# Gate and output chunks of three mixers in the wide form: 512 + 256 columns and a sum on VectorE

## The chip, the cores and the metric

One core of a Trainium2 chip runs the kernel. The metric is the device time of one execution in microseconds; before the change it is 2266.87 us, the median of three runs (2266.55 to 2266.92).

## What is computed

Two blocks over a sequence of 256 tokens of 1024 features, in float32. The first has an even and an odd mixer, each followed by a SwiGLU; the second has two layers of SwiGLU, layer norm, hybrid mixer, layer norm, SwiGLU, layer norm. The change touches the gate of the odd mixer and the last product of the hybrid mixers:

```python
def odd_mixer(h, w_in, out_norm, w_out, pos):
    z = h @ w_in
    ...
    g = z[..., 2 * nq + nv:]
    o = rmsnorm(retention(q, k, v), out_norm)
    o = o.reshape(B, S, nv).astype(h.dtype) * jax.nn.silu(g)
    return o @ w_out

def hybrid_mixer(x, w_in, ...):
    ...
    merged = (gates[:, :, 0] * (o_a @ w_br_a) + gates[:, :, 1] * (o_b @ w_br_b)
              + gates[:, :, 2] * (o_c @ w_br_c))
    return merged @ w_out
```

## The kernel before

Activations lie feature-major: 128 features on the partitions, 256 tokens along the free axis, 8 such tiles for 1024 features. Weights stream through the core once, in chunks of 128 x 1024 values that one output tile of 128 features needs, in the order of the list `ORDER`. SyncE loads a chunk into one of six raw buffers. ScalarE rounds it to the high part `whi` (`upper`, L1239) and VectorE forms the low part `wlo` = raw - high (`lower`, L2001), each in one of five buffers; a buffer comes free when the chunk five before it has been multiplied. Activations have a high and a low part too, side by side in `m.xx` (the hybrid mixer's merged tensor in `m.mx`).

A product is high x high + low x high + high x low. TensorE has two forms for it.

- Narrow (`mm3`, L454, used by `gemm_fm`, L471): per k step three matmuls of 256 columns into the same 256 columns of a PSUM bank: high weights by high activations, low weights by high, high weights by low. Three weight loads. One operand of the reader then holds the whole result.
- Wide (`mm2`, L459, used by `gemm_wide`, L480): per k step one matmul of 512 columns (high weights by both parts of the activations, side by side) and one of 256 (low weights by the high part). Two weight loads. The result is the sum of the two halves of a bank, which the reader has to add: by a reduction on VectorE (`both`, L1997), or, where it is added to the residual x, by two instructions (`add_wide`, L2037) in place of one (`add_one`, L2047).

`gemm_first` (L487) interleaves several output tiles over k, so that a stage can start on the first tiles of its input. `take` (L445) makes TensorE wait for the last reader of a PSUM bank before it is written again.

Each engine has a program of its own, whose order is written out by hand; they meet at semaphores. Where a mixer has work beside its weight chunks, it is put into generators that are advanced by one step after each chunk (`Sides`, L151), on each engine for itself.

**The odd mixer.** Its gate has 16 chunks `ow_g`, TensorE loop at L900, into banks 0 to 3 in turn. For chunk i VectorE (L2761) lowers a weight chunk, waits for the product, multiplies it by the row of 1/rms (L2774) and advances its generators; ScalarE raises a weight chunk and applies SiLU (L1680). Beside this run the four retention heads: head 0 begins at i = 0, head 1 at i = 7, head 2 at i = 14, head 3 in the output product. For a head, TensorE forms the scores at its first step and the outputs two steps later, for which it needs VectorE's product with the decay (L2732, L2733), and the sum of squares two steps after that, for which it needs VectorE's sum of ScalarE's squares (L1656, L1659, L2739, L2742). Later VectorE forms the reciprocal (L2757), the scaled outputs (L2749), their product with the gate (L2753) and their low part (L2022). The output product `ow_out` follows with `gemm_acc` (L525): its first chunk writes banks 0 to 3, two tiles to a bank, and takes each bank as it comes to it, after the last reader of gate chunks 12 to 15.

**The hybrid mixer.** In its last stage TensorE multiplies the eight chunks `mw_o`: tiles 0 to 2 interleaved by `gemm_first`, tiles 3 to 7 one by one (L1203). VectorE adds each tile to x (`norm_tile` with `add_one`, L3124) and prepares the layer norm in the same loop (L2124): after tile 2 it lowers three weight chunks, subtracts an estimate of the mean from all eight tiles (L2150, L2153) and forms the low parts of the raw input of the next stage (L2193); for tiles 3 to 7 it adds, lowers a weight chunk and forms a low part; after tile 7 it forms seven partial sums (L2180) and seven partial sums of squares (L2188) and one more low part. ScalarE squares the tiles and forms their high parts. TensorE goes on to the feed-forward stage on the raw input (`gemm_raw`, L578), whose k steps wait for those low parts, and after two tiles it forms the mean (`layer_norm`, L569), for which it waits for the last partial sum.

Of the kernel before, what the change touches and what calls it, by code (L numbers as in the profile page):

```python
# [433 lines left out]
def tensor_program(e, m):  # L434
# [10 lines left out]
    def take(b, *readers):  # L445
        for sig, *key in free[b]:
            w.wait_ge(s[sig], *key)
        free[b] = list(readers)
        return ps[b]
# [9 lines left out]
    def mm2(b, wh, wl, a, start):  # L459

        mm(b[:, :], wh, a.rearrange("p a b -> p (a b)"), start=start, stop=False)
        return mm(b[:, 0:256], wl, a[:, 0, :], start=False, stop=True)
# [8 lines left out]
    def gemm_fm(name, i, out, ah, al, st=None):  # L471
        wh, wl = weights(name, i)
        for k in range(8):
            if st is not None:
                w.wait_ge(s["xlo"], st, k)
            c = k * 128
            t = mm3(out, wh[:, c:c + 128], wl[:, c:c + 128], ah[:, k, :], al[:, k, :], k == 0, k == 7)
        t.then_inc(s["gemm"].h, s["gemm"].up(name, i))

    def gemm_wide(name, i, b):  # L480
        wh, wl = weights(name, i)
        for k in range(8):
            c = k * 128
            t = mm2(b, wh[:, c:c + 128], wl[:, c:c + 128], m.xx[:, k], k == 0)
        t.then_inc(s["gemm"].h, s["gemm"].up(name, i))

    def gemm_first(st, specs, wide=False, a=m.xx, last=None):  # L487

        wv = []
        for k in range(8):  # L490
            if k == 6 and last:
                last()
            w.wait_ge(s["xlo"], st, k)
            for n, (name, i, out) in enumerate(specs):
                if k == 0:
                    wv.append(weights(name, i))
                wh, wl = wv[n]
                c = k * 128
                if wide:
                    t = mm2(out, wh[:, c:c + 128], wl[:, c:c + 128], a[:, k], k == 0)  # L500
                else:
                    t = mm3(out, wh[:, c:c + 128], wl[:, c:c + 128], a[:, k, 0, :], a[:, k, 1, :], k == 0, k == 7)
                if k == 7:
                    t.then_inc(s["gemm"].h, s["gemm"].up(name, i))
# [356 lines left out]
    def odd():  # L861
        for cg in range(4):
            bq = [take(2 * (cg % 2) + tt, ("ract", "v", cg, tt)) for tt in range(2)]
            gemm_tm("ow_v", cg * 4, bq, xh, xl, 8, 2, 512, st="o")
            if cg == 0:
                rms_stats("o", RT=True)
        for i in range(8):
            for c in (2 * i, 2 * i + 1):
                gemm_wide("ow_qk", c, take(4 + c % 4, ("rdve", "qk0", c)))
        hb = [h1, h2]  # L870

        def head(h):
            w.wait_ge(s["rdve"], "qk", 2 * h + 1)
            b = take(5, ("rdve", "A", h))
            for d in range(2):
                mm(b[:, 0:256], m.okF[:, 2 * h + d, 0:128], m.oqF[:, 2 * h + d, :], start=d == 0, stop=d == 1)
            for d in range(2):
                t = mm(b[:, 256:384], m.okF[:, 2 * h + d, 128:256], m.oqF[:, 2 * h + d, 128:256], start=d == 0, stop=d == 1)
            t.then_inc(s["rps"].h, s["rps"].up("A", h))
            yield  # L880
            yield
            w.wait_ge(s["rdve"], "A", h)
            w.wait_ge(s["ract"], "v", 3, 1)
            for pr in range(2):
                b = take(6 + pr, ("ract", "o", h, pr))
                for q in range(2):
                    ec = h * 512 + (pr * 2 + q) * 128
                    ob = b[:, q * 256:q * 256 + 256]
                    mm(ob, m.ovT[:, 0, ec:ec + 128], m.oAT[:, h % 2, 0:256], start=q == 0, stop=False)
                    t = mm(ob[:, 128:256], m.ovT[:, 1, ec:ec + 128], m.oAT[:, h % 2, 256:384], start=False, stop=True)  # L890
                t.then_inc(s["rps"].h, s["rps"].up("o", h, pr))
            yield
            yield
            w.wait_ge(s["rdve"], "sq", h)
            b = take(5, ("ract", "root", h))
            mm(b[:, 0:256], m.ones, m.osq[:, 0, :]).then_inc(s["rps"].h, s["rps"].up("sum", h))
            for _ in range(4):
                yield

        for i in range(16):  # L900
            gemm_fm("ow_g", i, take(i % 4, ("rdve", "g", i))[:, 0:256], xh, xl)
            if i in (0, 7, 14):
                side.add(head(i // 7))
            side.step()
        readers = [[("xadd", "f1", p)] for p in range(4)]
        for c in range(12):
            h, k = c // 4, c % 4
            w.wait_ge(s["hlo"], "o", c)
            gemm_acc("ow_out", c, hb[h % 2][0], hb[h % 2][1], k, c == 0, readers)
            if c == 4:  # L910
                side.add(head(3))
            side.step()
        side.finish()
        gemm_last("ow_out", 12, lambda k: ("o", 12 + k), h2)

    def hybrid(l):
# [283 lines left out]
                product(br, p, take(1, ("merge", l, br, p, 0)), oh, tag, till)  # L1200
        side.finish()
        st = f"t{l}"
        gemm_first(f"g{l}", [(f"mw_o{l}", n, take(m.mo_bank[n], ("xadd", st, n))[:, 0:256]) for n in range(3)], a=m.mx)  # L1203
        for n in range(3, 8):
            gemm_fm(f"mw_o{l}", n, take(m.mo_bank[n], ("xadd", st, n))[:, 0:256], m.mx[:, :, 0, :], m.mx[:, :, 1, :])
            if n == 3:
                centre(st, 1)

# [768 lines left out]
def vector_program(e, m):  # L1977
# [19 lines left out]
    def both(dst, b):  # L1997

        return e.tensor_reduce(dst, b[:, :].rearrange("p (a b) -> p b a", a=2), AX, ALU.add)  # L1999
# [44 lines left out]
        w.wait_ge(s["xadd"], st, n, "part")  # L2044
        e.tensor_tensor(v, v, b[:, 256:512], ALU.add).then_inc(s["xadd"].h, s["xadd"].up(st, n))

    def add_one(st, n, alpha, gemm, bank):  # L2047
        residual(st)
        v = x[:, n, :]
        w.wait_ge(s["gemm"], *gemm)  # L2050
        e.scalar_tensor_tensor(v, v, alpha, ps[bank][:, 0:256], ALU.mult, ALU.add).then_inc(  # L2051
            s["xadd"].h, s["xadd"].up(st, n))

    def lower_x(st, gname, k):
        if gname is None:
            low(xl[:, k, :], x[:, k, :], xh[:, k, :], ("xhi", "xlo"), st, k)
# [633 lines left out]
    def odd():  # L2690
# [79 lines left out]
        for i in range(16):  # L2770
            if i < 15:
                chunk()
            w.wait_ge(s["gemm"], "ow_g", i)
            e.tensor_tensor(m.sg[:, i, :], ps[i % 4][:, 0:256], R[:, 0, :], ALU.mult).then_inc(  # L2774
                s["rdve"].h, s["rdve"].up("g", i))
            if i == 15:
                chunk()
            if i in (0, 7, 14):
                side.add(head(i // 7))
            side.step()  # L2780
# [9 lines left out]
    def hybrid(l):  # L2790
# [330 lines left out]
        for n in range(8):  # L3121
            if n == 2:
                chunk()
            norm_tile(f"t{l}", (f"l2g{l}", f"l2b{l}"), n, 3, add_one, (f"mw_o{l}", n), m.mo_bank[n], late=True)  # L3124
            if 3 <= n < 7:
                chunk()

# [325 lines left out]
```

## Time and profile before

| What | Value |
|---|---|
| Median of three runs | 2266.87 us |
| The profiled execution's own time | 2266.66 us |
| Its span, first to last instruction | 2264.9 us |
| TensorE busy, of the span | 2251.1 us, 99% |
| Weight loads busy, beside the matmuls | 2047.7 us, 90% |
| VectorE busy | 1781.2 us, 79% |
| ScalarE busy | 1285.3 us, 57% |
| TensorE's granted clock, mean | 0.999 |

Busy times are sums over the whole span, and the matmuls' ends are modelled. The chain of waits is followed back from the last instruction: at each step to what released it, or to the instruction before it on its engine. A row of the timeline gives the start and the length in microseconds, the engine, the line, the operation, what it writes and reads with the shapes, the number of instructions merged, and in brackets the idle time of the engine before it with what ended it.

### The profile page before, as it was taken

The page shows a single profiled execution, that of the slowest core. Times are in us where ns is not written, and L with a number is a line of the kernel's source. Part 1 is how long each engine was busy: PE and PEld are TensorE (multiplying, and loading weights), DVE is VectorE, ACT ScalarE, POOL GpSimd, SP SyncE. Part 2 cuts the span into 40 slices and gives each one's busy share as a digit, 9 for nine tenths or more (in the row PEclk, how much of TensorE's full clock was granted, in tenths as well). Part 3 has the DMA queues.
Part 4 walks back from the last instruction along what each step waited for, and adds up shares of the span by engine and source line. Part 5 has one row for each costly group of instructions (what it writes and reads, how often), then busy time and mean ns, then how long its engine had stood idle before and what let it go on. Part 6 is the DMA issues. An engine that isn't in the chain of part 4 may idle for free.

```text
span 2264.9 us, 37643 instructions
## 1 busy us (share of the span) xinstructions
PE 2251.1 (99%) x15119; PEld 2047.7 (90%) x15119; DVE 1781.2 (79%) x2713; ACT 1285.3 (57%) x2016; POOL 79.4 (4%) x96
## 2 busy tenths in 40 slices
PE   9999999999999999999999999999999999999998
PEld 8988889998888888999999888998889999998887
DVE  7899658879858876897679886698768976798854
ACT  7855455655445555585666554466545856565542
POOL 0022000002100000020000000000000200000000
PEclk9999999999999999999999999999999999999999
DMA  7466565456556665654455555566665543556663
GB/s 244 132 199 196 193 211 176 150 159 215 184 186 214 195 192 191 204 178 129 133 172 193 197 194 190 168 203 206 195 194 197 180 133 122 182 182 221 190 185 100
DMA packets 115084, 412.45 MB, mean 182 GB/s; under 512 B 12896, under 2 KB 14304, under 8 KB 114656
## 3 DMA queue, kind: packets, MB, share of 16 engines
q1 hardware_dynamic: 114480, 407.77, 55.9%
q8 instruction: 120, 1.97, 0.4%
q0 software_dynamic: 288, 2.10, 0.3%
q14 instruction: 52, 0.43, 0.1%
q10 hardware_dynamic: 144, 0.18, 0.0%
HBM read 408.96 MB, written 1.05 MB: 181 GB/s over the span
## 4 chain that ended last, share of the span: by engine, by line
PE 88%; DVE 8%; ACT 2%; issue 1%; DMA 0%; SPq 0%; POOL 0%; DVEq 0%; ACTq 0%
PE ps L452 87%; DVE wlo L2004 3%; DVE region L2796 1%; ACT whi L1244 1%; ACT region L1466 1%; DMA raw<-in_ew_c 0%; PE ps L715 0%; DVE region L2323 0%; DVE RX L2193 0%; DVE x L2051 0%; DVE region L2326 0%; DVE x L2200 0%; DVE region L2439 0%; DVE region L2466 0%; DVE region L2965 0%
## 5 line engine op out<-in xcount | busy, mean ns | idle before, releaser
L452 PE MATMUL ps<-xx,whi 128*128 128x512 f32 (+1 forms) x4504 | 1286.2, 352 | 3.2 <-DVE wlo L2004 2.2
L2004 DVE TENSOR_TENSOR wlo<-raw,whi 128x1024 fp32r<-128x1024 f32 (+3 forms) x772 | 925.2, 1207 | 266.7 <-ACT whi L1244 265.7
L1244 ACT ACTIVATE whi<-raw 128x1024 fp32r<-128x1024 f32 (+3 forms) x772 | 801.1, 1043 | 491.3 <-PE ps L452 481.1
L452 PE MATMUL ps<-xx,wlo 128*128 128x256 f32 x3696 | 1025.0, 277 | 0.0
L452 PEld LDWEIGHTS ps<-xx,whi 128*128 128x128 f32 x4504 | 794.4, 188 | 120.2 <-issue 2.8
L452 PEld LDWEIGHTS ps<-xx,wlo 128*128 128x128 f32 x3696 | 693.8, 188 | 0.4
L452 PE MATMUL ps<-H,whi 128*128 128x512 f32 (+1 forms) x2144 | 571.6, 338 | 0.1
L452 PE MATMUL ps<-H,wlo 128*128 128x256 f32 x1632 | 453.7, 278 | 0.0
L452 PEld LDWEIGHTS ps<-H,whi 128*128 128x128 f32 x2144 | 370.7, 188 | 45.1 <-issue 0.6
L452 PEld LDWEIGHTS ps<-H,wlo 128*128 128x128 f32 x1632 | 306.7, 188 | 0.1
L1999 DVE TENSOR_REDUCE t<-ps 128x256 f32<-128x512 f32 x320 | 219.5, 688 | 31.6 <-PE ps L452 31.2
L1393 ACT ACTIVATE H<-t 128x256 fp32r<-128x256 f32 x140 | 58.6, 419 | 81.2 <-DVE t L2353 31.9
L1428 ACT ACTIVATE t<-t 128x256 f32<-128x256 f32 x160 | 65.5, 410 | 64.9 <-DVE t L2395 35.8
L452 PE MATMUL ps<-region 128*128 128x128 f32 (+9 forms) x944 | 89.4, 272 | 0.0
L452 PE MATMUL ps<-RX,whi 128*128 128x258 f32 x480 | 88.9, 284 | 0.0
L452 PEld LDWEIGHTS ps<-region 128*128 128x128 f32 (+5 forms) x944 | 75.8, 158 | 6.7
L452 PE MATMUL ps<-whi,Hs 128*128 128x512 f32 x256 | 79.8, 392 | 0.0
L452 PE MATMUL ps<-whi,xx 128*128 128x512 f32 (+1 forms) x288 | 79.3, 360 | 0.0
L452 PEld LDWEIGHTS ps<-RX,whi 128*128 128x128 f32 x480 | 75.3, 190 | 0.2
L3170 POOL TENSOR_TENSOR t<-t,R 128x256 f32<-128x256 f32 x44 | 53.3, 1211 | 549.1 <-ACT t L1428 549.1
L2022 DVE TENSOR_TENSOR H<-t,H 128x256 fp32r<-128x256 f32 x150 | 62.2, 419 | 9.0 <-ACT H L1393 5.8
L452 PE MATMUL ps<-RX,wlo 128*128 128x258 f32 x240 | 68.0, 283 | 0.0
(316 smaller groups left out, 1592.4 us busy)
## 6 DMA issues: line engine op xcount, KB each, us to landing
raw<-in_sg SPq DMA_DIRECT2D x128, 512.0 KB, 4.2
raw<-in_su SPq DMA_DIRECT2D x128, 512.0 KB, 4.2
raw<-in_sd SPq DMA_DIRECT2D x128, 512.0 KB, 4.4
raw<-in_mw_g SPq DMA_DIRECT2D x48, 512.0 KB, 3.7
raw<-in_fg SPq DMA_DIRECT2D x44, 512.0 KB, 4.1
raw<-in_fu SPq DMA_DIRECT2D x44, 512.0 KB, 4.2
raw<-in_fd SPq DMA_DIRECT2D x32, 512.0 KB, 3.6
raw<-in_mw_a SPq DMA_DIRECT2D x24, 512.0 KB, 4.2
```

What stands on the lines that cost most here:

```text
L452: return e.matmul(out, lhsT, rhs, start=start, stop=stop, skip_group_check=True)
L1244: e.activation(m.whi[:, c % NHL, 0:cw], m.raw[:, c % NRAW, 0:cw], ACT.Copy).then_inc(s["whi"].h, s["whi"].up(c))
L1393: e.activation(H[:, j, 0, :], m.t2[:, j % 4, :], ACT.Copy, scale=-0.5 if raw(j) else 1.0).then_inc(s["hhi"].h, s["hhi"].up(st, j))
L1428: e.activation(g, g, ACT.Silu).then_inc(s["silu"].h, s["silu"].up(st, j))
L1466: e.activation(S[:, i, sl], S[:, i, sl], ACT.Exp, bias=st[:, 1, c:c + 1], accum_out=st[:, 2, c:c + 1]).then_inc(s["aact"].h, s["aact"].up( ...
L1999: return e.tensor_reduce(dst, b[:, :].rearrange("p (a b) -> p b a", a=2), AX, ALU.add)
L2004: e.tensor_tensor(m.wlo[:, c % NHL, 0:cw], m.raw[:, c % NRAW, 0:cw], m.whi[:, c % NHL, 0:cw].bitcast(F32), ALU.subtract).then_inc(s["wlo"] ...
L2022: e.tensor_tensor(dst, src, hi.bitcast(F32), ALU.subtract).then_inc(s[sig[1]].h, s[sig[1]].up(*key))
L2796: e.scalar_tensor_tensor(y[:, d:256], pr[:, 0:256 - d], pk(f"cw{l}", 12 * (3 - d) + i), y[:, d:256], ALU.mult, ALU.add).then_inc(s["cdve"] ...
L3170: e.tensor_tensor(g, g, m.R[:, 0, :], ALU.mult).then_inc(s["fnrm"].h, s["fnrm"].up(st, j))
```

## The change

The 16 gate chunks of the odd mixer and the 8 output chunks of each of the two hybrid mixers go from the narrow to the wide form. In the odd mixer VectorE adds the two halves by a reduction into the gate's buffer, after which the bank is free (signal `gsum`), and then multiplies in place; the bank's next writer waits for the reduction. In the hybrid mixers `add_wide` takes the place of `add_one`.

```diff
-    def gemm_wide(name, i, b):
+    def gemm_wide(name, i, b, a=m.xx):
         wh, wl = weights(name, i)
         for k in range(8):
             c = k * 128
-            t = mm2(b, wh[:, c:c + 128], wl[:, c:c + 128], m.xx[:, k], k == 0)
+            t = mm2(b, wh[:, c:c + 128], wl[:, c:c + 128], a[:, k], k == 0)
...
         for i in range(16):
-            gemm_fm("ow_g", i, take(i % 4, ("rdve", "g", i))[:, 0:256], xh, xl)
+            gemm_wide("ow_g", i, take(i % 4, ("rdve", "gsum", i)))
...
-        gemm_first(f"g{l}", [(f"mw_o{l}", n, take(m.mo_bank[n], ("xadd", st, n))[:, 0:256]) for n in range(3)], a=m.mx)
+        gemm_first(f"g{l}", [(f"mw_o{l}", n, take(m.mo_bank[n], ("xadd", st, n))) for n in range(3)], wide=True, a=m.mx)
         for n in range(3, 8):
-            gemm_fm(f"mw_o{l}", n, take(m.mo_bank[n], ("xadd", st, n))[:, 0:256], m.mx[:, :, 0, :], m.mx[:, :, 1, :])
+            gemm_wide(f"mw_o{l}", n, take(m.mo_bank[n], ("xadd", st, n)), m.mx)
...
-    def add_one(st, n, alpha, gemm, bank):
-        residual(st)
-        v = x[:, n, :]
-        w.wait_ge(s["gemm"], *gemm)
-        e.scalar_tensor_tensor(v, v, alpha, ps[bank][:, 0:256], ALU.mult, ALU.add).then_inc(
-            s["xadd"].h, s["xadd"].up(st, n))
...
             w.wait_ge(s["gemm"], "ow_g", i)
-            e.tensor_tensor(m.sg[:, i, :], ps[i % 4][:, 0:256], R[:, 0, :], ALU.mult).then_inc(
+            both(m.sg[:, i, :], ps[i % 4]).then_inc(s["rdve"].h, s["rdve"].up("gsum", i))
+            w.wait_ge(s["rdve"], "gsum", i)
+            e.tensor_tensor(m.sg[:, i, :], m.sg[:, i, :], R[:, 0, :], ALU.mult).then_inc(
                 s["rdve"].h, s["rdve"].up("g", i))
...
-            norm_tile(f"t{l}", (f"l2g{l}", f"l2b{l}"), n, 3, add_one, (f"mw_o{l}", n), m.mo_bank[n], late=True)
+            norm_tile(f"t{l}", (f"l2g{l}", f"l2b{l}"), n, 3, add_wide, (f"mw_o{l}", n), m.mo_bank[n], late=True)
```

The functions that it calls, as they are:

```python
    def both(dst, b):
        return e.tensor_reduce(dst, b[:, :].rearrange("p (a b) -> p b a", a=2), AX, ALU.add)

    def add_wide(st, n, alpha, gemm, bank):
        ...
        e.scalar_tensor_tensor(v, v, alpha, b[:, 0:256], ALU.mult, ALU.add).then_inc(
            s["xadd"].h, s["xadd"].up(st, n, "part"))
        w.wait_ge(s["xadd"], st, n, "part")
        e.tensor_tensor(v, v, b[:, 256:512], ALU.add).then_inc(s["xadd"].h, s["xadd"].up(st, n))
```

## Rows read from the trace of the kernel before

**Rows 1.** The page: busy times of the engines, and TensorE's clock in 40 slices.

```profile
PE 2251.1 (99%) x15119; PEld 2047.7 (90%) x15119; DVE 1781.2 (79%) x2713; ACT 1285.3 (57%) x2016; POOL 79.4 (4%) x96
...
PEclk9999999999999999999999999999999999999999
```

**Rows 2.** The chain of waits, layer 0's hybrid output: start, length, what.

```profile
1177.08 0.76 DVE x L2051 x2
...
1198.80 0.71 PE ps L452 x2
```

**Rows 3.** The table of waits, TensorE: us in total, times, longest.

```profile
PE ps L452 <- DVE R L2180: 0.8, 2, 0.4
```

**Rows 4.** Timeline of TensorE's weight loads: a wide pair of chunks, a narrow one.

```profile
1143.90 0.19 PEld L452 LDWEIGHTS ps<-xx,whi 128*128 128x128 f32 x1
...
1149.34 0.19 PEld L452 LDWEIGHTS ps<-H,whi 128*128 128x128 f32 x1
...
1160.44 0.19 PEld L452 LDWEIGHTS ps<-xx,whi 128*128 128x128 f32 x1
...
1166.09 0.19 PEld L452 LDWEIGHTS ps<-H,whi 128*128 128x128 f32 x1
```

**Rows 5.** Timeline of VectorE, layer 0's hybrid output and its norm.

```profile
1177.08 0.75 DVE L2051 SCALAR_TENSOR_TENSOR x<-x,ps 128x256 f32<-128x256 f32 x2 [2.73 <-PE ps L452]
...
1193.58 0.41 DVE L2051 SCALAR_TENSOR_TENSOR x<-x,ps 128x256 f32<-128x256 f32 x1
...
1198.34 0.41 DVE L2180 TENSOR_TENSOR R<-R,x 128x256 f32<-128x256 f32 x1
```

**Rows 6.** Timeline of VectorE, an add of two halves in a feed-forward stage.

```profile
232.57 0.41 DVE L2042 SCALAR_TENSOR_TENSOR x<-x,ps 128x256 f32<-128x256 f32 x1
233.02 0.42 DVE L2045 TENSOR_TENSOR x<-x,ps 128x256 f32<-128x256 f32 x1
```

**Rows 7.** Timeline of VectorE in the odd mixer: gate products and head 1's decay.

```profile
395.37 0.42 DVE L2774 TENSOR_TENSOR region<-ps,R 128x256 f32<-128x256 f32 x1 [1.70 <-PE ps L452]
...
406.08 0.42 DVE L2732 SCALAR_TENSOR_TENSOR region<-ps,region 128x256 f32<-128x256 f32 x1
406.42 0.28 DVE L2733 SCALAR_TENSOR_TENSOR region<-ps,region 128x128 f32<-128x128 f32 x1
...
413.45 0.43 DVE L2774 TENSOR_TENSOR region<-ps,R 128x256 f32<-128x256 f32 x1 [2.63 <-PE ps L452]
...
416.27 0.43 DVE L2774 TENSOR_TENSOR region<-ps,R 128x256 f32<-128x256 f32 x1 [0.21 <-PE ps L452]
...
419.53 0.42 DVE L2774 TENSOR_TENSOR region<-ps,R 128x256 f32<-128x256 f32 x1 [1.70 <-PE ps L452]
...
430.77 0.41 DVE L2774 TENSOR_TENSOR region<-ps,R 128x256 f32<-128x256 f32 x1
```

**Rows 8.** Timeline of VectorE, reductions of halves and the products after them.

```profile
120.82 0.68 DVE L1999 TENSOR_REDUCE t<-ps 128x256 f32<-128x512 f32 x1
121.61 0.42 DVE L2353 TENSOR_TENSOR t<-t 128x256 f32<-128x256 f32 x1
...
123.42 0.68 DVE L1999 TENSOR_REDUCE t<-ps 128x256 f32<-128x512 f32 x1
124.13 0.43 DVE L2395 TENSOR_TENSOR t<-t,R 128x256 f32<-128x256 f32 x1
```

**Rows 9.** The waits of the odd mixer's gate, 374 to 434 us, VectorE.

```profile
DVE region L2774 <- PE ps L452: 12.7, 8, 3.9
```

**Rows 10.** Timeline of ScalarE: the gate of chunk 9, the last square of head 1.

```profile
409.66 0.42 ACT L1680 ACTIVATE region<-region 128x256 f32<-128x256 f32 x1
...
411.75 0.63 ACT L1659 ACTIVATE region<-region 128x512 f32<-128x512 f32 x1
```

**Rows 11.** Timeline of TensorE's weight loads: the output matmuls of heads 1 and 2.

```profile
407.68 2.71 PEld L452 LDWEIGHTS ps<-region 128*128 128x128 f32 x16
...
431.94 2.71 PEld L452 LDWEIGHTS ps<-region 128*128 128x128 f32 x16
```

## The prediction

> **What bounds the kernel now.** The page comes first: TensorE is busy for 99% of the span, at full granted clock in every slice, VectorE for 79% [rows 1]. TensorE's own time looks like the price of everything, and VectorE's like cover. The chain of waits, read next, corrects this for the second half of the change: from 1177.08 us, where the hybrid mixer's output is added to x, it runs through VectorE's instructions and comes back to TensorE's matmuls only at 1198.80, at the layer norm's mean [rows 2]. The table of waits has TensorE waiting twice for VectorE's last partial sum, once in each layer, 0.4 us each [rows 3]. So VectorE's 79% is an average, and the change puts its new work into its fullest stretches. 0.2% (4.5 us) is about what a measurement of this kernel can tell from no change.
>
> **What the wide form saves on TensorE.** The trace holds both forms of a gate chunk side by side. Two wide ones run from the weight load at 1143.90 to the next work at 1149.34: 5.44 us, 2.72 each. Two narrow ones run from 1160.44 to 1166.09: 5.65 us, 2.825 each [rows 4]. A chunk saves 0.105 us; 16 gate chunks and 2 x 8 output chunks save 3.3 us if nothing else moves.
> A rule speaks against even this. The Trainium skill, TensorE: Matmul & The Clock Gate, section Back-to-back issue gap, gives an isolated warm matmul N/2.4 + 2.5 ns. By it a step of three narrow matmuls takes 327.5 ns and a wide step 325, an estimate of 0.6 us saved over all 256 steps. The rows differ (353 against 340 ns a step), and the sum goes by them; rival (d) has the other case.
>
> **Output chunks of the hybrid mixers.** TensorE ends the first three tiles together, and at 1177.08 VectorE starts on their adds, released by TensorE. It never waits for TensorE again in this stretch: its last add starts at 1193.58. The last partial sum starts at 1198.34 and ends at 1198.75 [rows 5], and TensorE resumes at 1198.80. The new form makes each add two instructions, the second waiting for the first. That pair exists elsewhere: it starts at 232.57 and 233.02, so it takes 0.45 us more a tile [rows 6]; the second is as long as the single add (0.42 against 0.41). Eight tiles: 8 x 0.45 = 3.6 us. Against it stand the three chunks in front of the stretch, 3 x 0.105 = 0.3 us. The other five chunks' gain only makes TensorE wait longer. Net +3.3 us a layer, **+6.5 us** for both. Layer 1 has the same order and the same wait [rows 3].
> Bounds: a second instruction that follows as closely as an independent one would cost 0.34 (406.08 to 406.42, after an instruction of 0.42 [rows 7]); with the widest gap that a dependent pair shows, 0.11 (120.82 + 0.68 to 121.61 [rows 8]), it costs 0.53. That is +4.8 and +7.9 for both layers. I take 0.45, from the same instructions on the same shapes.
>
> **Gate chunks of the odd mixer.** Each product becomes a reduction of both halves and then the product. In the feed-forward stage that pair starts at 123.42 and 124.13 [rows 8]: 0.71, taken as 0.72 with the spread of such pairs, 11.5 us over 16. VectorE is idle for 12.7 us before these products [rows 9], but not where it is needed. Up to product 5, 8.2 us of it lie before six products, and a little is left there. Product 5 then starts with TensorE, 6 x 0.105 = 0.6 us before 395.37. From there to product 15, at 430.77, VectorE waits for TensorE 2.63, 0.21 and 1.70 us, 4.54 in all [rows 7]. Ten products (5 to 14) add 7.2, so all of it is used up. One wait is new: ScalarE copies and squares head 1's output behind the gate of chunk 9, and needs 2.7 us from 409.66 to the end of the last square at 412.38 [rows 10]. They end 3.2 us after product 9 begins (0.45 and 2.7); VectorE, which has only that product, a lowering and the next pair in front of them, is there after 2.5, an estimate, and waits 0.65. Product 15's place comes at 430.77 - 0.6 + 7.2 - 4.54 + 0.65 = 433.5, and its reduction ends 0.69 later, at 434.2.
> Who waits: the first chunk of the output product writes with its last two tiles into bank 3, which holds gate chunk 15. TensorE gets to them six matmuls (6 x 0.118 = 0.7 us) before head 2's matmuls at 431.94 [rows 11], at 431.2; product 15 ends at 431.18 now, just in time. After the change the bank is free at 434.2, and all behind it is 2.9 to 3.0 us late: **+2.9 us**. TensorE's gain over the 16 chunks is in this already, since VectorE's queue sets the time. Within it lies an earlier stall, not to be added: head 1's decay product ends at 406.70 [rows 7], and TensorE wants it at 407.68 [rows 11]. Products 5, 6 and 7 delay it by 2.16, four gate chunks bring TensorE there 0.4 earlier, and 2.16 + 0.4 - 1.0 leaves about 1.5. Bounds: 2.0 if the new wait doesn't arise and the pair costs 0.69; 3.5 if it costs 0.79, less what then becomes idle again. Weights are lowered three to four chunks (8 us and more) ahead, and ScalarE already waits for these products, not the other way round, so later gates hold up neither; the weights' transfers go by TensorE's pace and see nothing.
>
> **Sum.** Profiled execution 2266.66 us (span 2264.9) + 6.5 + 2.9 = 2276.1; the median of the runs, 2266.87, lies 0.2 above that execution. Forecast 2276.1, +0.41%. The terms' bounds give 2273.5 to 2278.1.
>
> **Rivals.**
> (a) The cover holds: VectorE's additions lie beside other work everywhere, and only TensorE's 3.3 us count: 2263.4, inside 0.2%. For it speaks VectorE's 79% [rows 1]; against it the 21 us in which VectorE never waits for TensorE [rows 2, 5]. It needs 3.6 us of idle time there in each layer. Chance 0.05.
> (b) Only the hybrid mixers pay: product 15 is not what TensorE meets, or its lateness is made good, and the 16 gate chunks keep their 1.7: 2266.7 + 6.5 - 1.7 = 2271.5. For it, 12.7 us idle before the products [rows 9]; against it, none after 419.53 [rows 7]. Chance 0.08.
> (c) Only the odd mixer pays, the adds being absorbed in the tail of sums: 2266.7 + 2.9 - 1.7 = 2267.9. The tail has no idle time. Chance 0.02.
> (d) The wide form saves nothing, both streaming 768 columns a step. As VectorE sets the two kinds of stretch, only the 6 + 3 + 3 chunks ahead of them lose their gain: +1.3, 2277.4. The measured steps speak against it [rows 4]. The skill's page on TensorE named above would have it nearly so. Chance 0.04.
> (e) The second instruction of a pair follows as if independent (0.34, and 0.69 for the reduction): 1.8 less in the hybrid mixers and 0.3 in the odd one, 2274.0. The pairs on record show 0.45 and 0.71 instead [rows 6, 8]. The Trainium skill, VectorE: DVE Perf Modes, section The DRAIN you can't avoid, says that a semaphore after each instruction costs nothing, which would bring this case. Chance 0.04.
> (f) TensorE's clock falls after a stall of over 2 us. The trace shows 1.00 throughout and thus no price; if one chunk after each of four stalls ran at half speed, 4 x 2.7 = 11 us more: 2287. Chance 0.03.
> The forecast keeps 0.74. Range: down to 2271.4 to take in (b), up to 2278.6 for the terms' upper bounds and (d); (a), (c), (f) stay out. Slower by over 0.2%: forecast, (d), (e), (f) and half of (b), 0.89. Within: (a), (c), half of (b), and a hundredth taken off, 0.10. Faster by over 0.2% would need more than all that TensorE can save: 0.01.
>
> **What would show it.** Wide steps of 0.340 us in both places. TensorE waiting some 1.5 us before head 1's output matmuls and 2 to 3 us inside the first output chunk, for a reduction. In each hybrid layer, 24.9 us from the first add to the last partial sum instead of 21.3, and TensorE waiting 3 to 5 us in sum for normalised tiles and for that sum. Wrong if VectorE shows idle time there, if TensorE's waits stay near 0.4 us, or if a granted clock under 1.00 appears.

## The result, and the profile after

| | before | after |
|---|---|---|
| Median of five runs | 2266.87 us | 2282.51 us |
| Lowest and highest | 2266.55, 2266.92 | 2277.31, 2284.39 |
| Ratio, 95% interval | | 1.0061, 1.0045 to 1.0077 |
| Profiled execution, its span | 2266.66, 2264.9 | 2284.39, 2282.3 |

Slower, as forecast, but by 0.7% in place of 0.41%: 2282.51 lies 3.9 us above the range. A second set of six runs of the same kernel (e3_after_again below) gave a ratio of 1.0053 (1.0037 to 1.0068). All these runs count as undisturbed, and yet they fall into groups, which the rest needs. The runs of before are the five measured with the change and 101 from four sets beside the experiments:

| Kernel | quickest group | with +1.6 to 1.8 | 5.2 above these |
|---|---|---|---|
| before, 106 runs | 2266.53 to 2267.13 (80) | none | 2271.83 to 2272.10 (26) |
| after, 11 runs | 2276.96, 2277.09, 2277.31 | 2278.80, 2278.97 | 2282.20, 2282.34, 2282.51; 2284.24, 2284.39 |

The eleventh run after, 2286.73, lies 9.7 us above the quickest and was not profiled. The quickest group is 10.3 us above that of before: 2277.0. The forecast had 2276.1. All further comparisons are between quickest groups unless said otherwise.

The page after. VectorE has 18 us more than before, TensorE is still 99% busy, and the clock's row still shows nothing but 9s [rows 1].

```profile
PE 2258.5 (99%) x14863; PEld 2039.6 (89%) x14863; DVE 1799.5 (79%) x2745; ACT 1286.1 (56%) x2016; POOL 79.5 (3%) x96
...
PEclk9999999999999999999999999999999999999999
```

The rows that the change adds to the table of waits of TensorE (us in total, times, longest); before it, two waits of 0.4 us for the last partial sum were all that it had in these stretches [rows 3]:

```profile
PE ps L452 <- DVE RX L2186: 6.0, 4, 1.7
...
PE ps L452 <- DVE region L1999: 2.2, 1, 2.2
...
PE ps L452 <- DVE region L2726: 1.2, 1, 1.2
...
PE ps L452 <- DVE R L2173: 0.6, 1, 0.6
```

Every one is where the forecast put it: the normalised tiles' raw low parts (L2186) and the last partial sum (L2173) in the hybrid mixers, the reduction of the gate chunk in bank 3 (L1999, the 2.2 us) and head 1's decay product (L2726) in the odd one.

VectorE's timeline in hybrid layer 0 after the change: first add, one middle tile, the last partial sum.

```profile
1187.34 0.42 DVE L2042 SCALAR_TENSOR_TENSOR x<-x,ps 128x256 f32<-128x256 f32 x1 [2.42 <-PE ps L452]
1187.80 0.42 DVE L2045 TENSOR_TENSOR x<-x,ps 128x256 f32<-128x256 f32 x1
...
1204.59 0.41 DVE L2042 SCALAR_TENSOR_TENSOR x<-x,ps 128x256 f32<-128x256 f32 x1
1205.03 0.42 DVE L2045 TENSOR_TENSOR x<-x,ps 128x256 f32<-128x256 f32 x1
1205.37 1.22 DVE L2004 TENSOR_TENSOR wlo<-raw,whi 128x1024 fp32r<-128x1024 f32 x1
...
1212.11 0.41 DVE L2173 TENSOR_TENSOR R<-R,x 128x256 f32<-128x256 f32 x1
```

From the first add to the last sum it is 24.77 us (forecast 24.9, before 21.26 [rows 5]). The pair runs from 1204.59 and 1205.03 to 1205.37: 0.78 us from the first add to the next work, in place of 0.34.

So the mechanism stood, and the rest of the time had to be somewhere else. Two places turned up when the same instructions were followed through both traces.

**A step of 0.350 us.** The first feed-forward stage, 106 to 290 us, isn't touched by the change, yet the profiled execution lost 5.2 us in it. A wide step is one matmul of 512 and one of 256 columns, with their two weight loads. Here are two loads of that stage, 175 wide steps apart, first in the profiled execution of after:

```profile
228.33 0.19 PEld L452 LDWEIGHTS ps<-H,whi 128*128 128x128 f32 x1
...
289.58 0.19 PEld L452 LDWEIGHTS ps<-H,whi 128*128 128x128 f32 x1
```

and then in a second profile of the same kernel (the run e3_after_again below, 2276.96 us):

```profile
224.52 0.19 PEld L452 LDWEIGHTS ps<-H,whi 128*128 128x128 f32 x1
...
284.02 0.19 PEld L452 LDWEIGHTS ps<-H,whi 128*128 128x128 f32 x1
```

61.25 us against 59.50: 0.350 us a step against 0.340, in one kernel, at a granted clock of 1.00 in both. Some 522 steps of this stage run so: 5.2 us. The four profiled executions of this document that lie in an upper group (after, e4, e7, e13) have 0.350 us in this stage, the twelve others 0.340.

**Stretches at the lower clock.** The page's slices are 57 us long and hide them; windows of 4 us in the profiled execution after (columns: busy us of each engine, then granted clock, DMA share, GB/s):

```profile
436.00:440.00 4.00, 1.78 (x13) 1.38 (x12) 3.16 (x8) 1.98 (x4) 0.00 (x0) 1.00 0.41 131
440.00:444.00 4.00, 3.96 (x16) 3.52 (x17) 3.83 (x4) 1.79 (x3) 0.00 (x0) 0.62 0.37 108
444.00:448.00 4.00, 4.00 (x32) 3.86 (x32) 1.32 (x3) 2.98 (x5) 0.00 (x0) 0.96 0.87 285
...
2008.00:2012.00 4.00, 4.00 (x23) 4.00 (x23) 4.00 (x13) 1.42 (x3) 0.00 (x0) 0.62 0.30 107
```

TensorE does little from 436 to 440 us, waiting for bank 3. Behind that its clock is granted at 0.50, 1.2 GHz (the window from 442 to 444 has 0.50 throughout), for 3.4 us. Two windows lose 0.38 x 4 and 0.04 x 4 us of full clock, 1.7 us together, which is half of the 3.4. It comes again in hybrid layer 1, behind waits of 1.3 and 1.7 us. With TensorE always busy such a stretch costs 1.7 us.

### The profile page after: what moved, and what is told of

It is laid out like the page before. It is cut to its first block, busy times and chain, and to the rows that moved or that the text cites. A ratio compares the mean times of both kernels' runs of the same rounds, so it can differ in the third digit from the quotient of the medians.

```text
span 2282.3 us, 37155 instructions
## 1 busy us (share of the span) xinstructions
PE 2258.5 (99%) x14863; PEld 2039.6 (89%) x14863; DVE 1799.5 (79%) x2745; ACT 1286.1 (56%) x2016; POOL 79.5 (3%) x96
## 4 chain that ended last, share of the span: by engine, by line
PE 88%; DVE 9%; ACT 2%; issue 1%; DMA 0%; SPq 0%; POOL 0%; DVEq 0%; ACTq 0%
PE ps L452 87%; DVE wlo L2004 3%; DVE region L2791 1%; ACT whi L1244 1%; DMA raw<-in_ew_c 0%; PE ps L715 0%; ACT region L1466 0%; DVE x L2045 0%; DVE region L2316 0%; DVE RX L2186 0%; DVE x L2042 0%; DVE region L2319 0%; DVE x L2193 0%; DVE region L1999 0%; DVE region L2960 0%
## 5 line engine op out<-in xcount | busy, mean ns | idle before, releaser
L452 PEld LDWEIGHTS ps<-xx,whi 128*128 128x128 f32 x4376 | 778.4, 188 | 127.9 <-issue 2.7
L452 PEld LDWEIGHTS ps<-H,whi 128*128 128x128 f32 x2016 | 355.0, 188 | 53.7 <-DVE region L1999 2.7
L1999 DVE TENSOR_REDUCE t<-ps 128x256 f32<-128x512 f32 x320 | 219.5, 688 | 34.0 <-PE ps L452 33.0
```

The lines of the kernel that those rows point to most:

```text
L452: return e.matmul(out, lhsT, rhs, start=start, stop=stop, skip_group_check=True)
```

## The experiments

In the code below, `...` marks lines left out. The theory at this point: VectorE's queue sets +6.5 and +3 us; the two other effects come on top in some executions. The rivals: the 0.350 us step or the clock belongs to the wide form or to the changed program; or VectorE's work is covered and something else costs.

**1. Each half alone, the whole again, and TensorE's half alone.**

e1_hybrid_only takes the odd mixer's change back (against the changed kernel):

```diff
-            gemm_wide("ow_g", i, take(i % 4, ("rdve", "gsum", i)))
+            gemm_fm("ow_g", i, take(i % 4, ("rdve", "g", i))[:, 0:256], xh, xl)
...
-            both(m.sg[:, i, :], ps[i % 4]).then_inc(s["rdve"].h, s["rdve"].up("gsum", i))
-            w.wait_ge(s["rdve"], "gsum", i)
-            e.tensor_tensor(m.sg[:, i, :], m.sg[:, i, :], R[:, 0, :], ALU.mult).then_inc(
+            e.tensor_tensor(m.sg[:, i, :], ps[i % 4][:, 0:256], R[:, 0, :], ALU.mult).then_inc(
```

> The changed kernel with the odd mixer's gate chunks back in the narrow form; the hybrid mixers' output chunks stay wide. VectorE-bound theory: +6.5 us on the kernel before, about 2273.4 (2271.5 to 2275); the two layers' stretches from the first add to the last partial sum take 24.8 us each. Clock theory: stalls of 1.3 and 1.7 us in these stretches can be followed by a stretch of TensorE at the lower granted clock, worth about 1.7 us each time: up to 2276.8. Slow-rhythm theory (TensorE's wide step of 0.350 us in place of 0.340 in the first feed-forward stage, 5.2 us): if it belongs to the program, it is gone or there in all runs; if it belongs to the execution, single runs spread over 5 us. Rival, cover holds: 2265.3.

Quickest group 2273.76 to 2273.80: +7.1. Two runs stand 1.3 and 1.8 above it, two 5.0 above; ratio 1.0033 (1.0020 to 1.0045). The profiled one is that at 1.8, and its clock is at 0.50 twice: for 6.8 us in layer 0, with this window, and for 3.4 us in layer 1, from 1998.5 us.

```profile
1198.00:1202.00 4.00, 4.00 (x21) 4.00 (x20) 4.00 (x13) 1.76 (x3) 0.00 (x0) 0.50 0.36 123
```

e2_odd_only is the kernel before with that edit the other way round, in the odd mixer alone.

> The kernel before with the odd mixer's gate chunks alone in the wide form. VectorE-bound theory: +2.9 to +3.3 us, 2269.8 to 2270.2. Clock theory: the 2.2 us stall before the output product's bank 3 is followed by a stretch at the granted clock 0.50 and about 1.7 us more: 2271.7. Slow-rhythm theory: 5.2 us on top if the first feed-forward stage again steps at 0.350 us. Rival, cover holds: 2265.2.

Quickest group 2270.07, 2270.11: +3.4; ratio 1.0023 (1.0012 to 1.0034). Five runs stand at 2271.5 to 2272.4 and five at 2276.8 to 2277.1. So 10 of 12 have the 1.6 us, and the profiled one shows why, right behind the 2.2 us wait:

```profile
436.00:440.00 4.00, 4.00 (x19) 3.53 (x19) 2.44 (x3) 1.76 (x4) 0.00 (x0) 0.68 0.67 188
```

7.1 + 3.4 = 10.5 against 10.3 for the whole: the halves add up to within 0.2.

e3_after_again is the changed kernel with no edit.

> The changed kernel as it is, a second time, with a second profile. VectorE-bound theory: stalls and their places as in the first profile, spans apart only by the clock and the step. Clock theory: the granted clock falls to 0.50 again right behind a stall of about 2 us of TensorE (odd mixer, bank 3), and not necessarily in the same hybrid layer; single runs differ by about 1.7 us for each fall. Slow-rhythm theory: if tied to the program the first feed-forward stage steps at 0.350 us again and runs stay at 2277 to 2284; if tied to the execution the profile may show 0.340 and a time of 2277 to 2279.

Its profile has 0.340 us steps in the first feed-forward stage and no fall in the odd mixer, although the wait is the same: its waits, and the window behind them.

```profile
PE ps L452 <- DVE RX L2186: 6.0, 4, 1.7
...
PE ps L452 <- DVE region L1999: 2.2, 1, 2.2
PE ps L452 <- DVE region L2726: 1.3, 1, 1.3
```

```profile
436.00:440.00 4.00, 4.00 (x32) 3.84 (x31) 2.88 (x4) 3.36 (x6) 0.00 (x0) 1.00 0.68 202
```

This is the cleanest execution to hold against the one before: over the odd mixer it falls behind by 3.25 us, over hybrid layer 0 by 3.23, over layer 1 by 3.5 (there the clock was at 0.50 from 1999.8 to 2003.2 us, in the middle of the waits for VectorE, and cost 0.3). Forecast: 2.9, 3.27 and 3.27. The step of the first feed-forward stage and the fall of the clock differ between executions of one program; and a wait makes a fall possible, not certain.

e4_no_second_half keeps TensorE's wide form and gives VectorE back its single instructions, which read only the first 256 columns; high weights by low activations are left out of these chunks. Against the changed kernel:

```diff
-            gemm_wide("ow_g", i, take(i % 4, ("rdve", "gsum", i)))
+            gemm_wide("ow_g", i, take(i % 4, ("rdve", "g", i)))
...
-            both(m.sg[:, i, :], ps[i % 4]).then_inc(s["rdve"].h, s["rdve"].up("gsum", i))
-            w.wait_ge(s["rdve"], "gsum", i)
-            e.tensor_tensor(m.sg[:, i, :], m.sg[:, i, :], R[:, 0, :], ALU.mult).then_inc(
+            e.tensor_tensor(m.sg[:, i, :], ps[i % 4][:, 0:256], R[:, 0, :], ALU.mult).then_inc(
...
-            norm_tile(f"t{l}", (f"l2g{l}", f"l2b{l}"), n, 3, add_wide, (f"mw_o{l}", n), m.mo_bank[n], late=True)
+            norm_tile(f"t{l}", (f"l2g{l}", f"l2b{l}"), n, 3, add_one, (f"mw_o{l}", n), m.mo_bank[n], late=True)
```

> The changed kernel's TensorE work (wide form for the gate and output chunks), but VectorE reads only the first half of each bank by the single instructions of the kernel before; the product of low weights... the second half of each bank, high weights by low activations, is left out of the result. It measures what TensorE saves when VectorE adds nothing. Measured-step theory (0.105 us a chunk, 32 chunks): 2263.5, less up to 0.8 if the remaining waits for VectorE swallow the last chunks' gain, so 2263.5 to 2264.8. Rival (both forms stream alike): 2266.3 to 2266.9. Slow-rhythm theory, if tied to the change of TensorE's program: 2268 or more.

Quickest group 2265.18 to 2265.58: 1.4 us saved of the 3.3. Followed through the trace, 0.95 is saved in the odd mixer and 0.3 in each hybrid layer: what the first three output tiles bring. The five later tiles of a layer bring nothing, since TensorE waits for VectorE's queue even with no work added. In the odd mixer 16 chunks should have saved 1.7 us; a part of what is missing is shown with e5 below. The group lies 0.4 above the expected 2264.8. The rival of equal streaming (2266.3 or more) is out. VectorE's additions then cost 10.3 + 1.4 = 11.7 us. The ratio over all runs, 0.9998 (0.9988 to 1.0008), sees none of this: 6 of these 11 runs are in the upper group, and 8 of the 24 of before.

**2. A part of the chunks: is the price in the place?**

e5_odd_first_five and e6_odd_first_twelve, against the kernel before:

```diff
-            gemm_fm("ow_g", i, take(i % 4, ("rdve", "g", i))[:, 0:256], xh, xl)
+            if i < 5:
+                gemm_wide("ow_g", i, take(i % 4, ("rdve", "gsum", i)))
+            else:
+                gemm_fm("ow_g", i, take(i % 4, ("rdve", "g", i))[:, 0:256], xh, xl)
```

(and the same condition on VectorE; `i < 12` in the second).

> The kernel before with only the first five of the odd mixer's gate chunks in the wide form, where VectorE still has idle time before the products. VectorE-queue theory: the 5 x 0.6 to 0.72 us of new VectorE work are covered, TensorE gains 5 x 0.105 = 0.5 us, no new wait for VectorE and no fall of the granted clock: quickest runs at 2266.1 where those of the kernel before are at 2266.6. Rival (each pair costs TensorE something wherever it stands): 2267 or more. Both theories: a share of the runs 5.2 us higher, with the first feed-forward stage at 0.350 us a step.

2266.31 to 2266.60 in nine runs, two at 2271.6: 0.33 us quicker than before, no new wait. The sign is as expected, the gain 0.33 in place of 0.5. Weight loads of TensorE show where the rest went. Chunks 1 and 2 run between the scores and the outputs of head 0, chunks 3 and 4 behind the outputs; first the kernel before, then e5:

```profile
377.87 0.19 PEld L452 LDWEIGHTS ps<-xx,whi 128*128 128x128 f32 x1
...
383.52 0.19 PEld L452 LDWEIGHTS ps<-region 128*128 128x128 f32 x1
...
386.15 0.19 PEld L452 LDWEIGHTS ps<-xx,whi 128*128 128x128 f32 x1
...
391.80 0.19 PEld L452 LDWEIGHTS ps<-region,cst 128*128 128x128 f32 x1
```

```profile
377.77 0.19 PEld L452 LDWEIGHTS ps<-xx,whi 128*128 128x128 f32 x1
...
383.37 0.30 PEld L452 LDWEIGHTS ps<-region 128*128 128x128 f32 x2
...
386.01 0.19 PEld L452 LDWEIGHTS ps<-xx,whi 128*128 128x128 f32 x1
...
391.46 0.30 PEld L452 LDWEIGHTS ps<-region,cst 128*128 128x128 f32 x2
```

Both pairs take 5.65 us in the narrow form. In the wide form the first takes 5.60 and the second 5.45, so a chunk gains 0.025 or 0.1 us. The first pair's steps are 0.350 us apart, the second's 0.340. The same is seen in every profile with wide gate chunks: those right behind a head's scores step at 0.350 (in e3 some 40 of the mixer's 118 steps), while every wide step of the hybrid output chunks takes 0.340.

> The kernel before with the first twelve gate chunks of the odd mixer wide, the last four narrow. VectorE-queue theory: 4 x 0.72 = 2.9 us less is in front of product 15, so the 2.2 us wait for bank 3 is gone or under 0.3 us; the 1.3 us wait before head 1's outputs stays; +0.6 to +1.3 us, 2267.3 to 2268.0. Clock theory (the fall to 0.50 follows the 2.2 us stall): no run shows the extra 1.7 us, the granted clock stays 1.00 behind 431 us. Rival (the loss is spread over all sixteen chunks): three quarters of +3.4, 2269.2, and falls still in most runs.

Eight runs at 2267.91 to 2268.31, three at 2273.3 to 2273.5, none 1.6 above: +1.4 us. The last four chunks alone cost 2.0 of the 3.4, and with them the falls are gone. e12_odd_first_fourteen (`i < 14`) stands between:

> The kernel before with the first fourteen gate chunks of the odd mixer wide, the last two narrow. VectorE-queue theory: the wait for bank 3 is 2.2 - 2 x 0.72 + 2 x 0.1 = about 1.0 us (0.4 with twelve, 2.2 with sixteen); quickest runs at about 2269.1. Clock theory: a wait of 1.0 us is followed by a fall of the granted clock in fewer runs than one of 2.2 us (10 of 12 runs of the sixteen-chunk version lay 1.6 us above its quickest); if the length does not matter, again in most.

Nine runs at 2268.95 to 2269.09, two at 2274.4 and 2274.5: +2.3, no fall. The wait for bank 3, L2783 being the narrow product, in the tables of waits of e6, of e12, and of e2 with sixteen chunks:

```profile
PE ps L452 <- DVE region L2783: 0.4, 1, 0.4
```

```profile
PE ps L452 <- DVE region L2783: 1.4, 1, 1.4
```

```profile
PE ps L452 <- DVE region L1999: 2.2, 1, 2.2
```

It follows the number of pairs in front of product 15: 0.4, 1.4, 2.2. And no fall in 22 runs with 1.4 or 0.4, 10 in 12 runs with 2.2.

e7_hybrid_first_three makes only output tiles 0 to 2 wide:

```diff
-        gemm_first(f"g{l}", [(f"mw_o{l}", n, take(m.mo_bank[n], ("xadd", st, n))[:, 0:256]) for n in range(3)], a=m.mx)
+        gemm_first(f"g{l}", [(f"mw_o{l}", n, take(m.mo_bank[n], ("xadd", st, n))) for n in range(3)], wide=True, a=m.mx)
...
-            norm_tile(f"t{l}", (f"l2g{l}", f"l2b{l}"), n, 3, add_one, (f"mw_o{l}", n), m.mo_bank[n], late=True)
+            norm_tile(f"t{l}", (f"l2g{l}", f"l2b{l}"), n, 3, add_wide if n < 3 else add_one, (f"mw_o{l}", n), m.mo_bank[n], late=True)
```

> The kernel before with only the first three output tiles of each hybrid mixer wide and added in two instructions. VectorE-bound theory: 3 x 0.45 less 3 x 0.105 = 1.04 us a layer, 2.1 in all: 2268.7; the wait for the last partial sum stays 0.4 us and that for the normalised tiles grows from nothing to about 1. Rival (only tiles 3 to 7, whose adds TensorE's matmuls run beside, or the sum's end by other work, cost time): 2266.0 to 2266.7. Clock theory: with stalls under 1 us no fall, all runs in two groups at 2268.7 and 5.2 above.

Five runs at 2268.85 to 2268.93, six at 2274.0 to 2274.2, nothing between: +2.15, of 2.1 expected. In its trace TensorE falls 1.08 us behind in each layer. So a pair costs 0.45 less 0.105 a tile in front of the stretch.

**3. A wait made on purpose.** e13_pause adds idle work to the kernel before, in front of layer 0's last partial sum:

```diff
+                    if k == 7 and st == "t0":
+                        for q in range(5):
+                            e.tensor_tensor(R[:, 1, :], x[:, 0, :], x[:, 1, :], ALU.add).then_inc(
+                                s["pad"].h, s["pad"].up(q))
+                            w.wait_ge(s["pad"], q)
                     total(st, k, nz)
```

> The kernel before, all narrow, with five VectorE instructions that nobody needs, each waiting for the one before, in front of the last partial sum of hybrid layer 0. VectorE-bound theory: 5 x 0.44 = 2.2 us more on the path, TensorE's wait there 0.4 + 2.2 = 2.6 us, time 2268.9. Clock theory: the granted clock falls to 0.50 behind that wait in most runs, which lie 1 to 1.7 us higher still, 2270.6. Rival (the falls belong to the wide form or to the odd mixer, not to a wait): none here.

Lowest 2269.17 (+2.4), five at 2269.64 to 2269.73, one at 2270.89, and four at 2274.2 to 2275.2. Its wait, and the windows behind it, in the profiled run:

```profile
PE ps L453 <- DVE R L2186: 3.1, 2, 2.7
```

```profile
1206.00:1208.00 2.00, 1.54 (x5) 1.27 (x5) 1.88 (x3) 0.22 (x1) 0.00 (x0) 0.58 0.03 8
1208.00:1210.00 2.00, 2.00 (x11) 1.91 (x10) 1.43 (x3) 1.41 (x4) 0.00 (x0) 0.57 0.51 162
```

All these chunks are narrow here, and no gate chunk is touched, so a fall needs neither the wide form nor the odd mixer; it came behind the wait. By the trace this one cost 0.7 us. By the times of the others, which were not profiled, it mostly costs 0.5 and once 1.7, less than forecast. That follows from where in the 3.4 us TensorE is busy, I take it; it was not separated.

**4. Work given to GpSimd.** e10_relieved is the changed kernel with the gate's product with R, and the hybrid layers' sums of squares, on GpSimd; e11_best has the first with the narrow hybrid chunks.

```diff
-            w.wait_ge(s["rdve"], "gsum", i)
-            e.tensor_tensor(m.sg[:, i, :], m.sg[:, i, :], R[:, 0, :], ALU.mult).then_inc(
-                s["rdve"].h, s["rdve"].up("g", i))
...
-                    squares(st, k)
...
+    for i in range(16):
+        w.wait_ge(s["rdve"], "gsum", i)
+        e.tensor_tensor(m.sg[:, i, :], m.sg[:, i, :], m.R[:, 0, :], ALU.mult).then_inc(s["gpo"].h, s["gpo"].up(i))
...
+            e.tensor_tensor(m.t8[0], m.t8[0], m.t8[k], ALU.add).then_inc(s["sqp"].h, s["sqp"].up(st, k))
```

> The changed kernel, all 32 chunks wide, with two pieces of VectorE's work given to GpSimd, which is idle there: the gate's product with R in the odd mixer (VectorE keeps the reduction, about 0.61 us from start to start against 0.34 for the old product), and the hybrid layers' seven sums of squares. VectorE-queue theory: odd mixer 10 x 0.27 = 2.7 us of new work against 4.5 us of idle time, so no wait for bank 3 and -0.3 to -1.0 us; hybrid layer +3.3 less 6 x 0.35 = +1.2 us; in all 2266.7 - 0.6 + 2.4 = 2268.5 against 2277.0 of the changed kernel's quickest runs. Rival (the wide form costs TensorE time by itself, or GpSimd's and VectorE's accesses hinder each other): 2272 or more. Clock theory: no fall, since no wait reaches 2 us.

> Odd mixer's gate chunks wide with the product on GpSimd, hybrid output chunks narrow as in the kernel before, their seven sums of squares on GpSimd. VectorE-queue theory: odd -0.3 to -1.0 us; each hybrid layer gains its wait of 0.4 us for the last partial sum and no more, unless the sum of squares on GpSimd (7 instructions of 1.2 us, the last after ScalarE's last square) is late, about 1 us then. 2265.3, quicker than both kernels. Rival: GpSimd's sums are late and TensorE waits for them: 2267 to 2268.

Both missed, by far: 2287.6 to 2289.5, ratio 1.0090 (1.0077 to 1.0103), and 2279.4 to 2280.4 with one at 2288.4, ratio 1.0058 (1.0042 to 1.0074). e10_relieved, VectorE's timeline in layer 0, and then GpSimd's:

```profile
1199.04 1.22 DVE L2006 TENSOR_TENSOR wlo<-raw,whi 128x1024 fp32r<-128x1024 f32 x1
1200.17 0.96 DVE L2187 SCALAR_TENSOR_TENSOR RX<-x,pk,RX 128x256 fp32r<-128x256 f32 x1
...
1209.09 0.47 DVE L2187 SCALAR_TENSOR_TENSOR RX<-x,pk,RX 128x256 fp32r<-128x256 f32 x1
1209.49 1.86 DVE L2174 TENSOR_TENSOR R<-R,x 128x256 f32<-128x256 f32 x4
```

```profile
1199.65 1.20 POOL L3222 TENSOR_TENSOR t<-t 128x256 f32<-128x256 f32 x1 [1.60 <-ACT t L1316]
...
1208.03 0.86 POOL L3222 TENSOR_TENSOR t<-t 128x256 f32<-128x256 f32 x1 [1.60 <-ACT t L1316]
```

The low part L2187 takes 0.96 us where GpSimd's add runs beside it and 0.47 where it doesn't. The Trainium skill, SBUF — State Buffer, section SBUF: two separate sides, says that a VectorE instruction with two inputs in SBUF and a GpSimd instruction that reads SBUF exclude each other for their whole length. These rows agree that the two hinder each other, and don't show that it is for the whole length: the low part takes 0.49 us more beside the add, and the add 1.20 us where the last row has 0.86. Four low parts of this layer are hit, and the five subtractions behind tile 2 take 2.85 us where e3 has 1.76. And taking the squares out of the tail saves little: they had filled the gap between dependent sums. Four sums alone take 1.86, some 0.47 apart; interleaved, a sum and a square took 0.67 together. In the odd mixer ScalarE's high parts now come later, VectorE waits 1.51 us for them before head 1's decay product where it was 0.79 in e3, and TensorE waits 2.1 us for that product and 2.4 for bank 3. The expected "no fall" failed too: the clock of e10 is at 0.50 for 3.4 us three times, from 436.6, 1204.6 and 2010.2 us, and that of e11 for 6.8 us from 435.9. What these falls cost was not separated from the waits. Freeing one queue lengthened another's chain.

**5. Two more, on what was still open.** e14_odd_nine (`i < 5 or 8 <= i < 12`):

> The kernel before with nine gate chunks of the odd mixer wide: 0 to 4 and 8 to 11, where the version with five showed VectorE idle before products 10 and 12 (2.25 and 1.70 us). VectorE-queue theory: the four new pairs, 4 x 0.72 = 2.9 us, fit into that idle time, no wait for head 1's decay product (products 5, 6, 7 are single) and none for bank 3; TensorE gains 4 x 0.105 = 0.4 us on top of the 0.33 of the first five: quickest group at 2266.0 against 2266.75 of the kernel before. Rival (any pair behind product 5 makes some chain late): 2266.8 or more.

Nine runs at 2266.64 to 2266.77 beside 2266.57 to 2267.13 of before: 0.17 us quicker in the medians of the groups, half of what e5 gave. Through its trace TensorE is 0.54 us ahead before head 2, and 0.16 behind it:

```profile
PE ps L452 <- DVE region L2783: 0.2, 1, 0.2
```

Product 15 comes no earlier, so what TensorE gains in front of bank 3 is handed back there. e5 is the best version, by 0.33 us, or 0.015%: less than pays for the second form.

The entry into the wide form of the first feed-forward stage, in the kernel before: at 105.40 us TensorE takes a weight chunk for whose low part it has waited 0.14 us. e9_nudge_entry puts a small instruction in front of that lowering, e15_nudge_more one of 96 columns:

```diff
+            if st == "f0" and p == 3:
+                for _ in range(1):
+                    e.tensor_tensor(m.dly[:, :], pk(gname, 0, 8), pk(gname, 0, 8), ALU.add)
             if p < 4:
                 chunk()
```

> The kernel before with one extra VectorE instruction on 8 columns (about 0.06 us) in front of the lowering of the weight chunk with which TensorE enters the wide form of the first feed-forward stage. Theory: which of the two step lengths (0.340 or 0.350 us) this stage keeps is decided at that entry, by tens of nanoseconds; then the share of runs at +5.2 us changes from 8 in 24, towards none or towards all, while the quicker group moves by under 0.1 us. Rival (something that holds for the whole execution decides it): the share stays at a third to a half, both groups 0.05 to 0.1 us later.

> As the version with the small extra VectorE instruction, now 96 columns instead of 8, so that TensorE enters the wide form about 0.2 us later than in the kernel before instead of 0.1. Entry theory: the share of runs with 0.350 us steps (18 of 62 runs of the kernel before, 8 of 11 with the small nudge) is again another one; the two groups stay 5.2 us apart. Rival (the shares are chance, one in three whatever the entry): 3 or 4 of 11.

8 of 11 and 6 of 10 runs are 5.2 us up, against 26 of 106 of the kernel before. (One more execution of the second took 4568.87 us; nothing explains it.) Fourteen of 21 where a quarter was to be expected is hardly chance. Eight versions whose instructions up to this stage are those of the kernel before (e2, e4 to e7, e12 to e14) have 30 of 89, so a share of a third comes without any nudge; 14 of 21 is well above that as well. The moment of entry very likely moves the odds. What decides a single execution isn't shown: the gap in front of the first load of the chunk was 0.37 us in executions of both kinds.

## Why the prediction was right and wrong

- **What bounds it**: right. The chain through VectorE in the hybrid mixers and the waits in both places came as written. e7 priced a part of it, and e13 lengthened the same chain without the change.
- **The wide form saves 0.105 us a chunk**: right in the hybrid mixers. In the odd mixer, where "wide steps of 0.340 us in both places" was named as a sign, the chunks behind a head's scores step at 0.350 and save 0.025 us, nearly rival (d)'s case. The whole 3.3 us were rightly not counted: without any work for VectorE only 1.4 came through (e4). Rival (d) as a whole is out, since it needed 2266.3 or more there.
- **Hybrid, +6.5**: 3.2 and 3.5 in the profile of e3, 7.1 us by the times of e1; of the latter, some 0.4 may lie elsewhere: in e1's profile TensorE is 0.6 us behind the one of before at 290 us already, in code that the change doesn't touch. The pair took the 0.45 more of [rows 6], and rival (e) is out.
- **Odd, +2.9**: 3.25 in the trace, 3.4 in the times. Bank 3 was free for TensorE at 434.48 in e3 where 434.2 was forecast. The contained wait was 1.3 us (1.5 forecast). Some luck is in the closeness: product 5 came 0.43 us earlier and not 0.6, VectorE still waited 0.40 us for TensorE where nothing was to be left, and its new wait for ScalarE was 0.31 and not 0.65, so that errors of both signs met. Rivals (a), (b) and (c) are out by e1 and e2.
- **The sum**: 2276.1 forecast, 2277.0 for an execution with neither of the other effects. Had the median been one of these, it would have been inside the range.
- **Where it failed, first**: the step "the median of the runs, 2266.87, lies 0.2 above that execution", which took the spread of the three runs shown for that of the kernel. The kernel has a second group 5.2 us up, in a quarter of its executions; none of the five runs of before fell into it and three of the five of after did. That is the larger part of the miss, 5.2 of 6.4 us. It arises in a stage that the change doesn't touch; whether the change moves its odds (5 of 11 after, 26 of 106 before) these few runs don't show.
- **Second**: rival (f). I gave the clock's fall 0.03 and priced it at 11 us for four stalls. It is frequent (10 of 12 runs of e2) and cheap, 0.3 to 1.7 us, since it mostly lasts 3.4 us and in the profiles of the changed kernel follows one or two of the waits, not all four. A granted clock under 1.00 was named as a sign of being wrong, and it appeared. With a chance of a half and 1.7 us the range would have reached 2280, and 2282.51 would still have been outside.

Left open: what picks the step length in an execution, and why it is 0.350 behind a head's scores; why the same 2.2 us wait was followed by a fall in 10 of 12 runs of e2 and, by their times, in some 5 of 11 of the full change; and whether a lone wait of 1.4 us never leads to one (in the hybrid layers waits of 1.3 and 1.7 us together did).

## What to carry to other kernels

Price a VectorE instruction by where it stands in VectorE's queue, not by VectorE's share: the same pair cost nothing in the odd mixer's first five chunks, about 0.5 us each in its last four, and 0.4 in the hybrid tiles. When a change makes TensorE wait where it didn't, as here for 1.3 us and more, look at its granted clock in windows of a few microseconds: the page's slices hid falls that cost 1.7 us. And look at the single times before using a median: a kernel that jumps by 5 us from one execution to the next needs some ten runs, compared group by group, before 0.3% means anything.

## What was not expected of the hardware

- One and the same sequence of wide steps (512 + 256 columns) runs in two rhythms: weight loads alternately 0.113 and 0.227 us apart, or 0.117 to 0.120 and 0.230 to 0.233. It keeps the one it enters with through 525 steps, at full granted clock, and loses it when the form of the matmuls changes. In the odd mixer the rhythm goes by the place: 0.350 us a step right behind a head's scores in every profile, and 0.340 elsewhere but for the chunks behind head 1's outputs in e6, e10 and e12.
- The granted clock fell to 0.50 behind waits of 1.3 to 2.7 us, mostly for 3.4 us (6.8 us in e1 and in e11), and the same wait in another execution was followed by none.
- A VectorE instruction on 128 x 256 values in SBUF takes 0.96 us in place of 0.47 when a GpSimd add of 128 x 256 runs beside it.
